# Two programs for eight cores, one per role: the first core of a sequence takes 2176 rows, the second 1920 rows and a prefix of 2176

## The reference

```
h = rmsnorm(x); [u_pool | u_rnn | u_gate | g_pool | g_rnn] = h @ W_in   # 512 + 4 x 1024 columns
y_pool = pool_mixer(u_pool) @ W_pool_out          # trailing means of 2, 4, 8, 16 rows
v = conv4(u_rnn);  r, i = sigmoid(v @ W_a), sigmoid(v @ W_x)            # 8 blocks of 128
a = sigmoid(lam) ** (8 r);  s_t = a_t s_{t-1} + sqrt(1 - a_t^2) i_t v_t # recurrence over rows
y_rnn = (s * gelu(u_gate)) @ W_rnn_out
x = x + (sigmoid(g_pool) y_pool + sigmoid(g_rnn) y_rnn) @ W_o
x = x + (silu(rmsnorm(x) @ W_gate) * (rmsnorm(x) @ W_up)) @ W_ffn_out   # 2816 wide
out = rmsnorm(x)
```

## Time and profile before

| | us |
|---|---|
| median of three runs (lowest, highest) | 1067.36 (1065.96, 1069.72) |
| the profiled execution, device time | 1073.55 |
| its span on the slowest core, core 5 | 1071.9 |
| its span on the other cores | 1056.8 to 1070.1 |

### The profile page before, as it was taken

How to read it: one execution, slowest core, us unless ns; L and a number is a source line. 1 busy time by engine, 2 the same in 40 slices (tenths; PEclk the granted TensorE clock), 3 DMA queues, 4 the chain that set the end, 5 groups by cost and what they waited for, 6 DMA issues and landing times.

```text
span 1071.9 us, 13859 instructions; the slowest of 8 cores (1056.8 to 1071.9 us)
## 1 busy us (share of the span) xinstructions
PE 979.6 (91%) x4592; PEld 442.9 (41%) x4592; DVE 702.4 (66%) x646; ACT 462.2 (43%) x507; POOL 284.9 (27%) x463
## 2 busy tenths in 40 slices
PE   1874698898899999999999999999999999999996
PEld 0431243343344444444444444444445444444442
DVE  2977998779969667955385787655487344443336
ACT  2677987666878653723441444000135210111012
POOL 2543444233534342302210221200234210111001
PEclk9977998999999988999999999999999999999998
DMA  9688766964685777771563667895463664654403
GB/s 213 184 133 187 150 141 115 221 131 84 138 192 149 171 174 185 172 201 20 88 107 51 109 136 161 164 245 128 70 173 83 101 108 68 99 88 62 86 1 158
DMA packets 73446, 140.64 MB, mean 131 GB/s; under 512 B 22688, under 2 KB 25120, under 8 KB 73376
## 3 DMA queue, kind: packets, MB, share of 16 engines
q0 software_dynamic: 37328, 66.73, 41.2%
q1 hardware_dynamic: 36048, 73.02, 21.5%
HBM read 177.08 MB, written 25.17 MB: 189 GB/s over the span
## 4 chain that ended last, share of the span: by engine, by line
PE 83%; ACT 5%; DMA 3%; issue 3%; DVE 3%; SPq 1%; POOL 1%; POOLq 0%; ACTq 0%; DVEq 0%
PE ps L600 61%; PE ps L1007 14%; PE ps L962 5%; DMA big<-xp 3%; PE ps L779 2%; PE ps L681 1%; DVE big L764 1%; ACT big L802 1%; DVE big L662 1%; ACT big L783 1%; SPq L672 1%; DMA big<-w_in_b 1%; POOL big L660 0%; ACT big L655 0%; ACT big L786 0%
## 5 line engine op out<-in xcount | busy, mean ns | idle before, releaser
L600 PE MATMUL ps<-big 128*128 128x512 bf16 x3200 | 725.6, 387 | 29.3 <-ACT big L831 12.4
L600 PEld LDWEIGHTS ps<-big 128*128 128x128 bf16 x3200 | 316.3, 99 | 423.0 <-issue 82.7
L989 ACT ACTIVATE big<-ps 128x1024 f32<-128x1024 f32 x44 | 45.0, 1023 | 314.6 <-PE ps L600 314.6
L1007 PE MATMUL ps<-big 128*128 128x512 bf16 x704 | 156.7, 379 | 1.6 <-DVE big L994 1.6
L991 DVE SCALAR_TENSOR_TENSOR big<-big,ps 128x1024 f32<-128x1024 f32 x44 | 53.6, 1218 | 119.3 <-ACT big L989 119.3
L764 DVE SCALAR_TENSOR_TENSOR big<-ps,big 128x1023 f32<-128x1023 f32 (+6 forms) x102 | 123.5, 1215 | 5.2 <-PE ps L600 0.4
L1012 DVE SCALAR_TENSOR_TENSOR big<-ps,big 128x1024 f32<-128x1024 f32 x80 | 97.1, 1222 | 44.5 <-PE ps L1007 44.0
L662 DVE SCALAR_TENSOR_TENSOR big<-big 128x1024 bf16<-128x1024 f32 (+1 forms) x64 | 83.3, 1302 | 33.2 <-POOL big L660 16.7
L1007 PEld LDWEIGHTS ps<-big 128*128 128x128 bf16 x704 | 68.9, 98 | 84.8 <-issue 2.0
L655 ACT ACTIVATE big<-big 128x1024 bf16<-128x1024 f32 x64 | 67.4, 1054 | 83.2 <-DVE big L1012 49.0
L591 POOL DMA_DIRECT2D big<-w_fi_b x88 | 47.5, 548 | 133.8 <-PE ps L600 131.9
(11 more groups left out here) (74 smaller groups left out, 689.8 us busy)
## 6 DMA issues: line engine op xcount, KB each, us to landing
big<-w_fi_b POOLq DMA_DIRECT2D x88, 256.0 KB, 7.8
big<-w_in_b POOLq DMA_DIRECT2D x80, 256.0 KB, 5.8
big<-xc SPq DMA_DIRECT2D x32, 512.0 KB, 5.4
big<-xp SPq DMA_DIRECT2D x16, 512.0 KB, 10.7
sp_t<-big SPq DMA_DIRECT2D x16, 512.0 KB, 6.7
big<-sp_t SPq DMA_DIRECT2D x16, 512.0 KB, 7.6
sp_thr<-big SPq DMA_DIRECT2D x16, 512.0 KB, 4.1
big<-sp_thr SPq DMA_DIRECT2D x16, 512.0 KB, 8.5
```

The lines of the kernel that those rows point to most:

```text
L600: r = e.matmul(pap(g, half * 512, half * 512 + 512), lhsT=w[:, kc, :], rhs=rhs_fn(kc, half), start=(kc == 0), stop=(kc == nk - 1))
L1007: r = e.matmul(pap(g, c * 512, c * 512 + 512), lhsT=act.h()[:, 1024 * i + t * 128:1024 * i + t * 128 + 128], rhs=wo.h()[:, 1024 * i + c * ...
```

## The change

There are two programs now, and each core picks one at its start: every engine loads a `role` word from DRAM into a register and branches on it. Role 0 (cores 0, 2, 4, 6) has no prefix: rows 0 to 1023 are its segment A and rows 1024 to 2175, 1152 of them, its segment B. Role 1 (cores 1, 3, 5, 7) keeps the prefix segments P0 and P1 (rows 0 to 2047). Its segment A is rows 2048 to 3071, of which the first 128 are prefix too (norm, recurrence and the last 16 of them for the pooling, but no output), and B is rows 3072 to 4095. So role 0 does 2176 rows of everything, role 1 does 4096 rows of recurrence and 1920 rows of the rest.

A `Span` says how a segment is cut. A product of 1152 columns is three matmuls of 384 columns, each in a bank of its own, so it takes three banks; one of 896 columns is 384 and 512; a recurrence over 1152 rows is 512, 512 and 128. PSUM is handed out by single banks (`PLACES`: where a group of 1, 2 or 3 banks may begin) and a transpose takes one bank. Each role has its own table in `NOMS`, thus its own order, and its own layout of the scratchpad. The 32 matmuls that brought the 16 rows before a second core's first row to the pooling (L846) and the flag (L815) are gone.

```diff
-    "NA": (32.5, 1.09), "N1": (-12.6, 14.56), "NB": (159.8, 5.11), "R": (30.0, 14.2),
...
+SPLIT = 2176
...
+        "N0": (7.1, 1.55), "NA": (20.9, 1.26), "N1": (-42.5, 19.11), "NB": (125.9, 6.68),
...
+    PLACES = {1: (7, 6, 5, 4, 3, 2, 1, 0), 2: (6, 0, 4, 2, 3), 3: (0, 3, 5)}
...
+class Span:
+    def __init__(self, seg, r0, n, lo=0):
+        self.seg, self.r0, self.n, self.lo, self.m = seg, r0, n, lo, n - lo
+        self.thirds = self.m == 1152
+        if self.thirds:
+            self.parts = [(384 * i, 384 * i + 384, 512 * i) for i in range(3)]
+        else:
+            self.parts = [(lo, 512, lo), (512, n, 512)]
+        self.nb = -(-n // 512)
...
+    if second:
+        spP0, spP1 = Span(None, 0, 1024), Span(None, 1024, 1024)
+        spA, spB = Span(0, 2048, 1024, 128), Span(1, 3072, 1024)
+        NSET, CAP = 4, 1024
+    else:
+        spA, spB = Span(0, 0, 1024), Span(1, 1024, 1152)
...
+    def product(b, sp, src, prio, after=(), nk=8, base=0):
+
+        g = PG(sp.nb)
+        v = src.h(nk)
+        st = src.n // nk
+        for i, (a, z, po) in enumerate(sp.parts):
+            a, z = a - base, z - base
+            o = mm_part(b, g, i, po, lambda kc, a=a, z=z: v[:, kc, a:z], z - a,
+                        [src.keys(k * st + 2 * a, k * st + 2 * z) for k in range(nk)], prio, after, nk)
...
+    def proj_all(b, sp, hT, prio, first=0):
+
+        g = PG(sp.nb)
+        v = hT.h(8)
+        for i, (a, z) in enumerate(sp.chunks):
+            a = max(a, first)
+            mm_part(b, g, i, a, lambda kc, a=a, z=z: v[:, kc, a:z], z - a,
+                    [hT.keys(k * 2 * sp.n + 2 * a, k * 2 * sp.n + 2 * z) for k in range(8)], prio)
+        return g
...
-        def rnn_unit(j, hT, p, state_only, last_prefix=False, halo=True, split=False):
...
-            g, _ = proj(b, hT, p)
...
+    def rnn_unit(j, sp, hT, p, state_only, more=True, split=False):
...
+        N = sp.n
+        U, V, A = SU[u].sub(0, 4 * N), SV[u].sub(0, 4 * N), SA[u].sub(0, 4 * N)
+        b = block(env.w_in_b, 4 + j, 8)
+        g = proj_all(b, sp, hT, p)
...
+    if second:
+        stage("N0")
+        norm_in(spP0, hP0, *NOM["N0"], lands=lands, via="dve")
+        stage("NA")
+        norm_in(spA, hA, *NOM["NA"])
+        more_constants()
+        stage("N1")
+        norm_in(spP1, hP1, *NOM["N1"], via="dma")
+        stage("R0")
...
+    else:
+        stage("NA")
+        norm_in(spA, hA, *NOM["NA"], lands=lands, via="dve")
+        more_constants()
...
+        plans = [plan(env, role, NOMS[role]) for role in range(2)]
...
+        def streams(name, e):
+            with e.register("role_" + name) as r:
+                e.reg_load(r, env.role)
+                with e.If_eq(r, 0):
+                    stream(name, plans[0], e)
+                with e.Else():
+                    stream(name, plans[1], e)
...
-        m["xc"] = np.ascontiguousarray(x[b, h * TOK:(h + 1) * TOK, :])
-        m["xp"] = np.ascontiguousarray(x[b, 0:TOK, :]) if h == 1 else np.zeros((TOK, D), np.float32)
...
+        in_maps.append(dict(common, x=x[c // 2], role=np.full((1, 1), c % 2, np.int32)))
...
```

More of the change, by code:

```diff
@@ L107, in op @@
     def op(self, eng, fn, reads=(), writes=(), prio=0.0, cost=0.1, sem=None, work=0.0, table=None,
-           pg_w=None, pg_r=(), ring=None, after=(), half=None):
+           pg_w=None, pg_r=(), ring=None, after=(), part=None):
         o = Op(eng, fn, prio, cost)
@@ L183, in run @@
         pe_warm, pe_streak = False, 0.0
-        pairs = [None] * self.npairs
+        banks = [None] * 8
         left = {}
@@ L247, in may_alloc @@
             for light in (False, True):
-                if light and sum(1 for g in pairs if g is not None and id(g) in loose and left[id(g)] > 0) >= 2:
+                if light and len({id(g) for g in banks if g is not None and id(g) in loose and left[id(g)] > 0}) >= 2:
                     return False
@@ L265, in run @@
                     continue
[L266 removed]
+                room = {}
                 cands = []
@@ L303, in run @@
             if o.alloc:
-                prev = pairs[pi]
-                if prev is not None:
-                    have = {d.idx for d in o.deps}
-                    for r in prev.readers:
+                have = {d.idx for d in o.deps}
+                for prev in banks[pi:pi + o.pg.nb]:
+                    for r in prev.readers if prev is not None else ():
                         if r.idx not in have:
+                            have.add(r.idx)
                             o.deps.append(r)
-                pairs[pi] = o.pg
-                o.pg.pair = pi
+                banks[pi:pi + o.pg.nb] = [o.pg] * o.pg.nb
+                o.pg.bank = pi
             cost = o.cost
@@ L443, in __init__, with like @@
         self.load = None
+class Span:
[7 more added lines that the diff above has]
+        self.nb = -(-n // 512)
+        self.chunks = [(q, min(q + 512, n)) for q in range(0, n, 512)]
+    def like(self, ap):
+        return ap.rearrange("p (k t) -> p k t", k=3) if self.thirds else ap
@@ L1209 @@
     for c in range(8):
-        b, h = c // 2, c % 2
-        out[b, h * TOK:(h + 1) * TOK, :] = res.results[c]["out"]
+        a, z = (0, SPLIT) if c % 2 == 0 else (SPLIT, SEQ)
+        out[c // 2, a:z, :] = res.results[c]["out"][0:z - a]
     return out
```

1331 lines of the change are left out of this document (668 added, 663 removed), and 13 rows, old and new, of tables (NOM, NOMS).

## The result

The changed kernel takes 1029.54 us (median of 4 runs, 1027.85 to 1030.66), 0.9636 of the kernel before (95% interval 0.9611 to 0.9661). The forecast was 1024, within 1004 to 1054. The profiled execution took 1029.49 us.

What follows compares the result with a forecast made beforehand. The prefix recurrence (VectorE nearly full) was taken to bound the first 300 us, TensorE the rest. Role 1, ending last: 1071.9 - 50.8 + 4 + 3 = 1028 span, + 1.65 - 6.2 = 1024 us; range 1004 to 1054.

Steps and rivals of the forecast that it cites:

- TensorE's work: Matmuls of each role if nothing waited: role 1 893.8 us, 50.8 less than before; role 0 925.3, 19.3 less.
- Rival (c): Granted clock's low stretch, 300 to 450 us, twice as long: 1034, 9 in 100; held to the end: 1180, 5.
- The branch: Kernel start: register loads from DRAM and the jump cost each role 3 us, bounds 0 and 4.5.
- Role 1's front: Up to the 16th prefix scan: ends near 287 us, its loss growing by 4 to 103; bounds 0 and +17.
- rival (b): Role 1's front, 50 to 100 us, shrinks by more than its work, gaining about 15 us: 1009; 17 in 100.
- TensorE should be full from there on: Sign for role 1 behind its 16th prefix scan: TensorE full at 0.216 us per 512 columns, 0.162 per 384.
- What role 1 loses behind its front: Role 1 after its front: losses kept from the old kernel, 18 us and 10 in the last stretch.
- Role 0's losses: Whole of role 0: 32 + 26 + 18 + 10 + 3 us on 925, span 1014, bounds 988 and 1055.
- the tie of 107 against 107: Role 0 up to its seventh unit: TensorE and VectorE each have 107 us of work; 26 us loss given.
- after that TensorE has the more work everywhere: Role 0 behind its seventh unit: TensorE sets the pace, with only the old kernel's 18 us lost.
- rival (a): Role 0 ends last, convolution and scan holding it back for the old 99 us: median 1050; 17 in 100.
- The last term: From role 1's span to the median: 1028 + 1.65 - 6.2 = 1024.

Runs made afterwards that it cites:

- exchanged branches: Changed kernel with the two branches exchanged, so that role 1 follows the test directly and role 0 is jumped to: 1041.1 us.
- hoisted head: Changed kernel with SP's eleven first transfers (eight row tiles among them) issued ahead of register load and branch, a few buffers moved: 1023.9 us.
- three forms: The hoisted head as first made (1023.9 us), with first row tiles ahead of norm weights and constants (1024.1), and with four row tiles (1022.1).
- four tiles: The hoisted head with four row tiles instead of eight ahead of the branch (NHEAD = 7 for 11): 1022.1 us.

## Why the prediction came out as it did

**Right in their terms.** TensorE's work: 0.162 us was taken for 384 columns, 0.163 measured. Three-bank groups in FB cost nothing: on core 0 TensorE waits 1.86 us at FB's beginning and not again in its gate and up. VectorE's work ahead of the 16th prefix scan: forecast 13.4 us less; windows of core 5 give 240.1 us to 297.5 before and 225.4 to 279.9 after, 14.7 less (five of the 19 pooling passes there are of segment B and full width, not 896 to 912).

```profile
0.00:297.50 297.50, 221.08 (x1042) 98.65 (x1043) 240.11 (x258) 211.81 (x243) 120.39 (x189) 0.93 0.74 155
```

```profile
0.00:279.90 279.90, 204.61 (x987) 95.64 (x988) 225.40 (x238) 213.32 (x242) 116.28 (x183) 0.92 0.74 161
```

Rival (c) did not come: from 700 to 1000 us the granted clock is 1.00 on all role 0 cores and 0.99 to 1.00 on those of role 1, with TensorE busy for 294 to 298 of the 300 us. It is lower (0.90 and 0.93 on core 0) in 250 to 350 us, where TensorE itself waits. The Trainium skill's rule (TensorE: Matmul & The Clock Gate, Seeing it yourself) that a die stays at 13/16 while three of its cores are dense does not agree with that execution.

**The branch was mis-sized.** Forecast 3 us for both roles, with 4.5 as the upper bound. It is 1.5 us for role 0 (first issue at 2.56, 1.06 before) and some 8 more for role 1 by its spans (exchanged branches: 8.5 and 7.9; the 13.1 of the hoisted head is no measure of it, since the tiles come earlier there than without a jump). The step took one packet of the instruction queue as the price of the jump and counted the first issue alone; behind it SP stood another 4.69 us, POOL came at 10.97, and ACT got its constants at 20.23. The Trainium skill (Runtime: NRT & Kernel Launch, Instruction fetch mechanics) says that a taken branch out of the fetched pages stalls on a fetch; the 3.7 us between the two roles' first vector instructions agree with it, and the exchange shows that it goes with the place, not with the role.

**Role 1's front was mis-sized the other way.** The 16th scan was forecast near 287 us and ended at 279.9 on core 5 (278 to 280 on all), in spite of the late start. The step let VectorE's idle time stand as it was. It fell from 57.4 to 54.5 us, though the first 50 us alone added 7.6: between 200 and 250 us it went from 12.8 to 2.5. Core 5, before and after:

```profile
200.00:250.00 50.00, 46.69 (x216) 20.80 (x215) 37.25 (x36) 30.39 (x28) 16.06 (x27) 1.00 0.75 172
```

```profile
200.00:250.00 50.00, 45.54 (x223) 21.29 (x222) 47.51 (x43) 42.91 (x41) 18.54 (x27) 1.00 0.79 175
```

That is rival (b), the front shorter than its work, in another place than the one named there. With the head hoisted the scan ends at 263.7 on that core, 34 us before the old 297.5.

**What role 1 loses behind its front was mis-sized, too.** The sign "TensorE should be full from there on" did not come: it stands for 9.4 to 10.9 us between 400 and 450 us (0.8 before), where the mix of segment A runs among the recurrence of B. By the prediction's own costs core 5 lost 98.5 us up to the 16th scan (given 99 + 4 + 3 = 106), 24.3 behind it (given 18) and 8.7 in the last 10 (given 10). So the errors nearly cancel, by luck: role 1 lost 1025.4 - 893.8 = 132 us, forecast 134.

**Role 0's losses: the step that failed.** Forecast 89 us, measured 1027.9 - 925.3 = 103. Its head was as forecast (28 to 30 us lost in the first 50; forecast 32). From 50 to 150 us it stood idle for 8.4 us on core 0 and lost 13 by the prediction's costs on core 2, whose trace holds every matmul; 26 were given: the tie of 107 against 107 was harmless. But "after that TensorE has the more work everywhere" was wrong, and with it the 18 taken over from the old kernel: between 150 us and the last 10 us core 2 lost 49, half of it (24) between 250 and 400 us, where the mix of the first span runs among the recurrence of the second (core 0 idles there for 19.6 us), and 13 between 550 and 700, where the wait for a weight near 675 is 5.4 of it. So role 0 ends level with role 1; the slowest core is of role 0 in seven of the eight executions of the changed kernel, as in rival (a), though not by its mechanism and far from its 1050.

What the runs settle of 250 to 400 us: neither the place of w_o on the queue, nor that of the passes moved on VectorE, nor a seventh of the traffic of 300 to 350 us (180 against 210 GB/s on core 0), nor eight additions on VectorE is the limit by itself; the waits moved or shrank, and the spans stayed. What is left is that recurrence and mix run there as one chain through TensorE, ACT, POOL, VectorE and eight banks, and that ACT is the link without gaps ahead of the longest wait. That it sets the stretch is not shown: no run took away a bank or work from ACT, and the cause stays open.

**The last term.** Role 1's forecast span was 1028, the slowest core's is 1027.9. That is luck: it is a core of role 0, for which 1014 was forecast; role 1's slowest took 1025.4. From the 1028, 6.2 us were taken, since the execution profiled before lay that far above its median. The one profiled now lies at its median, 1029.5, which is most of the 5.5 us between forecast and time.

**The best version** is the hoisted head: 1023.9, 1024.1 and 1022.1 us in three forms that can't be told apart, 0.960 (0.957 to 0.964), 0.959 (0.956 to 0.962) and 0.960 (0.955 to 0.965) of the kernel before, against 0.9636 (0.9611 to 0.9661).

## What to carry to other kernels

Two programs behind one test don't start alike: the one that is jumped to pays on every engine, so put there the role with slack, and issue what both need ahead of the test. When cores have different work, work out the losses of each one's own stretches: here role 1's 31 us less of work were all but eaten by 29 us more of losses. A wait that names an engine is moved easily: before believing it, look what that engine itself waits for and what waits next, and judge by the waits of the stretch and the span together, since a later wait can take a gain back.

## What the runs showed of the hardware

A jump over the other role's program delayed the first vector instruction by 3.7 us and POOL's first transfer by 8 (10.97 against 3.13); with the head ahead of the branch both came later still (8.3 and 15.5 us on core 1), with four tiles as with eight. A program that was left alone still moved: role 0's waits near 675 us, 4.5 to 7.9 us on its four cores, fell to 1.3 or less when role 1 started earlier and buffers changed places, without a change in its own order.
